# Three moves in a two-block transformer kernel: a multiply ahead of six weight splits, a weight split ahead of a routing step, and an expert's gather behind the slot scatters

## The chip, the cores and the metric

The kernel runs on one core of one Trainium2 chip. The metric is the device time of one execution in microseconds (us). Before the change it is 2412.04 us, the median of three runs (2407.6 to 2413.93).

## What is computed

Two transformer blocks follow each other on 512 tokens of width 1024, in float32. The first block has a recurrent half and an attention half whose outputs are normed and joined, a cross attention to a memory of 256 rows, and a mixture of 32 experts with two experts for each token. The second block (two layers) is not touched by the change. Cut to what matters here:

```python
y_rnn = recurrent_group(xr, xg, ...)             # gelu(xg) * h, h from a linear recurrence
y_att = chunk_band_attention(q, k, v, rel_bias)
mixed = concatenate([rms_norm(y_rnn, gn_rnn_w), rms_norm(y_att, gn_att_w)])
x = x + mixed @ w_out
x = x + memory_cross_attention(rms_norm(x, ln2_w), rms_norm(mem, mem_norm_w), xq_w, xk_w, xv_w, xo_w)
h = rms_norm(x, ln3_w)
g_p, g_idx = top_k(softmax(h @ w_group + b_group), 1)          # one of 4 groups
e_p, e_idx = top_k(softmax(logits of the 8 experts of that group), 2)
for each expert e: rows of its tokens are gathered, (silu(rows @ w_gate[e]) * (rows @ w_up[e])) @ w_down[e]
x = x + the two experts' rows of each token, weighted with g_p * e_p
```

## The kernel before, in words

Activations lie transposed, with the features on the 128 partitions and the 512 tokens along the free dimension. Each large product is made of three matmuls on a high and a low part of both operands. A weight therefore goes through a fixed chain: SyncE loads it into `ring`, ScalarE copies a high part of it, VectorE subtracts to get the low part, and only then TensorE reads it. Each engine has its own program, which is a fixed list in the order in which the code is written, and semaphores tie the lists together. An instruction that waits holds everything that is written behind it on its engine.

**The stage before the first attention.** The weights come in units of 256 columns (numbered g). `unit_high(g)` is ScalarE's copy (line 1245), `unit_low(g)` VectorE's subtraction (line 1237). Units 10 to 13 make the memory's keys, units 14 to 17 its values, units 18 and 19 are split for later. TensorE's list is here: units 10 to 13, one matmul that sums the squares of the recurrent half (`rms("gn_rnn")`, line 1976), then units 14 to 17 (`token_unit`, line 1967). ScalarE's list is: the high part of 15, two copies of results, `root(1)` that makes `rstd` of that sum (lines 2224 and 2225, with a load of a function table ahead of each), two tiles copied, then the high part of 16. VectorE's list is the low parts 12 to 19, and behind that of 16 the four multiplies of `G` by `rstd` (line 2167). These feed ScalarE's copies `high(...)` (line 2229) inside the attention. A unit's load is issued by SyncE when the low part of the unit two before it is done.

**The start of the experts.** `moe_tensor` (TensorE) computes the router's logits, turns the rows of `H`, counts the tokens of each expert in bank 6 (line 473, semaphore `routed` 3), and makes the lists of tokens in bank 7 (line 479, `routed` 4). Then it turns the rows of `X` (line 458), turns the gathered rows of expert 0 (`turn_x`, line 488, semaphore `x_turned`) and runs the blocks of the experts (`unit`, line 498). A block has four gate and up units, after the fourth of which it turns the next expert's rows. `moe_vector` (VectorE) picks the experts, waits for `routed` 3, computes each token's rank and the mask `AT_RANK` (lines 604 to 608), which the product of line 479 waits for, then takes the low part of unit 1 (`weights_low(1, 2)`, line 562) and waits for `routed` 4. Then it writes `idx` (line 612) and the slots of tokens beyond 128 for one expert (lines 615 to 641, semaphore `slots_done`). `moe_gpsimd` (GpSimd) gathers expert 0's rows into `XB` (`gather`, line 400). When these are turned it gathers those of expert 1, stores four lists (line 411), waits for `slots_done`, issues eight indirect stores of tokens (line 415), and goes on with the gathers of experts 2 and up, each when the rows of the expert before it are turned. All of GpSimd's transfers are in one queue (q0). SyncE's loads are in another (q1).

SyncE's program of this stage (`moe_sync`) loads the gate weights of expert 2 when two low parts are done (line 354, `ew_low` 2), and its up weights when four are (`ew_low` 4), with a row of final-norm weights (`FROW`, line 362) behind them.

Of the kernel before, what the change touches and what calls it, by code (L numbers as in the profile page):

```python
# [17 lines left out]
ALU = mybir.AluOpType  # L18
# [10 lines left out]
HC = HALF // P  # L29
# [6 lines left out]
EXPERTS = GROUPS * EPG  # L36
# [77 lines left out]
def build(nc, A, out):  # L114
    with ExitStack() as ctx:
        def sb(name, shape, dt=F32):
            return ctx.enter_context(nc.sbuf_tensor(name, shape, dt))
# [33 lines left out]
        rstd = sb("rstd", [P, T])  # L151
# [6 lines left out]
        def const(name, n=P):  # L158
            return konst[:, CK[name]:CK[name] + n]

        def col(name, i=0, p=P):
            return cols[0:p, C1[name] + i:C1[name] + i + 1]
# [4 lines left out]
        Q, K, G = QKVG[:, 0:4, :], QKVG[:, 4:8, :], QKVG[:, 12:16, :]  # L167
# [22 lines left out]
        a_sq, a_add, a_stat, a_rstd = sem("x_squares"), sem("x_squares_added"), sem("x_stat"), sem("x_rstd")  # L190
        a_hn, a_hi, a_lo = sem("x_normed"), sem("x_normed_high"), sem("x_normed_low")
# [59 lines left out]
        idx = sb("idx", [P, EXPERTS], U32)  # L251
# [51 lines left out]
        def e_low(u):  # L303
            return EW[u % 3][:, 4:8, :]
# [16 lines left out]
        x_turned, x_high, x_low = sem("x_turned"), sem("expert_x_high"), sem("expert_x_low")  # L321
# [66 lines left out]
        def moe_gpsimd(pool, st):  # L388
            st.do(pool.iota(ids[:, :, :], [[T, 2], [P, TT]], base=0, channel_multiplier=1))
            st.do(pool.memset(absent[:, :], ABSENT))  # L390
            st.wait()
            pool.dma_start(slot_dram[HEAD * P:DUMMY, :].rearrange("(p n) o -> p (n o)", p=P), absent[:, :]).then_inc(scattered, 16)
            pool.dma_start(routw[:, :, :], A["router_w"].rearrange("(k p) n -> p k n", p=P)).then_inc(s_rout, 16)
            pool.dma_start(routb[:, :], bass.AP(A["router_b"].tensor, 0, [[0, P], [1, NR]])).then_inc(s_rout, 16)
            pool.wait_ge(res_done, 16)
            st.do(pool.memset(XB, 0.0))
            st.wait()

            def gather(i, index):
                pool.indirect_dma_start(XB, None, rows_dram, bass.IndirectOffsetOnAxis(index, 0), bounds_check=SLOTS - 1, oob_is_err=False).then_inc(xb_landed, 16)  # L400

            def store(index):
                pool.indirect_dma_start(y_dram, bass.IndirectOffsetOnAxis(index, 0), YB[:, :, :].rearrange("p a n -> p (a n)"), None, bounds_check=SLOTS - 1, oob_is_err=False).then_inc(y_stored, 16)

            pool.wait_ge(mask_done, 3)
            pool.wait_ge(rows_stored, 16 * TT)
            gather(0, idx[:, 0:1])
            pool.wait_ge(x_turned, 1)
            gather(1, idx[:, 1:2])
            for n in range(HEAD):  # L410
                pool.dma_start(slot_dram[n * P:(n + 1) * P, :], idx[:, EXPERTS - HEAD + n:EXPERTS - HEAD + n + 1]).then_inc(scattered, 16)
            pool.wait_ge(slots_done, 1)
            for w in range(2):
                for t in range(TT):
                    pool.indirect_dma_start(slot_dram, bass.IndirectOffsetOnAxis(slots[:, w, t:t + 1], 0),
                                            ids[:, w, t:t + 1], None).then_inc(scattered, 16)
            for i in range(2, EXPERTS - 1):
                pool.wait_ge(x_turned, i)
                gather(i, idx[:, i:i + 1])
                if i >= LAG:  # L420
                    pool.wait_ge(y_a, i - LAG + 1)
                    store(idx[:, i - LAG:i - LAG + 1])
            pool.wait_ge(scattered, 16 * (2 * TT + 5))
            extra = pool.value_load(table_u[0:1, 60:61], min_val=1, max_val=OVER + 1)
            with pool.Fori(0, extra) as j:
                pool.dma_start(idx_more[:, 0:1], slot_dram[bass.ds((j + LAG) * P, P), :]).then_inc(idx_landed, 16)
                pool.dma_start(idx_more[:, 1:2], slot_dram[bass.ds(j * P, P), :]).then_inc(idx_landed, 16)
                wait_counted(pool, idx_landed, j * 32 + 32)
                wait_counted(pool, x_turned, j + EXPERTS - 1)
                gather(j, idx_more[:, 0:1])  # L430
                wait_counted(pool, xb_landed, j * 16 + EXPERTS * 16)
                wait_counted(pool, y_a, j + EXPERTS - LAG)
                store(idx_more[:, 1:2])
                wait_counted(pool, y_stored, j * 16 + (EXPERTS - LAG) * 16)
            for n in range(LAG):
                pool.dma_start(idx_more[:, 2 + n:3 + n], slot_dram[bass.ds((extra + n) * P, P), :]).then_inc(idx_landed, 16)
            wait_counted(pool, idx_landed, extra * 32 + LAG * 16)
            for n in range(LAG):
                wait_counted(pool, y_a, extra + EXPERTS - LAG + n)
                store(idx_more[:, 2 + n:3 + n])  # L440
# [114 lines left out]
        def moe_vector(dve, st):  # L555
# [4 lines left out]
            def weights_low(u, count, b=None):  # L560
                dve.wait_ge(ew_high, count)
                dve.tensor_tensor(e_low(u), e_raw(u, b), as_f32(e_high(u)), ALU.subtract).then_inc(ew_low, 1)  # L562
# [28 lines left out]
            for w in range(2):  # L591
# [7 lines left out]
            flat_hots = hots.rearrange("p w t n -> p (w t) n")  # L599
            step(dve.tensor_tensor(hot_ids.rearrange("p w t n -> p (w t) n"), flat_hots,  # L600
                                   const("slot", 2 * TT)[:, :, None].to_broadcast([P, 2 * TT, EXPERTS]), ALU.mult))
            dve.wait_ge(routed, 3)
            before = bank[6][:, 0:TT * EXPERTS].rearrange("p (t n) -> p t n", n=EXPERTS)
            step(dve.tensor_tensor(hot_rank, hots, before[:, None, :, :].to_broadcast([P, 2, TT, EXPERTS]), ALU.mult))
# [2 lines left out]
            step(dve.tensor_reduce(rank[:, :, None], flat_rank, AX.X, ALU.add))  # L607
            st.tell(dve.tensor_tensor(AT_RANK, const("count")[:, None, :].to_broadcast([P, 2 * TT, P]),
                                      rank[:, :, None].to_broadcast([P, 2 * TT, P]), ALU.is_equal), mask_done)
            weights_low(1, 2)  # L610
            dve.wait_ge(routed, 4)
            st.tell(dve.tensor_scalar(idx[:, :], bank[7][:, 0:EXPERTS], float(ABSENT), None, ALU.add), mask_done)

# [618 lines left out]
        def unit_low(dve, st, g):  # L1232

            ks, nc_ = k_chunks(g), unit_cols(g)
            w = WHL[g % 2]
            dve.wait_ge(wh_done, g + 1)
            st.tell(dve.tensor_tensor(w[:, 1, 0:ks, 0:nc_], raw_half(g)[:, :, 0:nc_], as_f32(w[:, 0, 0:ks, 0:nc_]), ALU.subtract), wl_done)  # L1237
# [805 lines left out]
        def _(dve):  # L2043
            st = Steps(dve, dve_own)
# [114 lines left out]
            dve.wait_ge(s_biasd, 32)  # L2159
            for m in range(1, HC):  # L2160
                add_squares(DC, m, HC)
            for g in range(12, 20):
                unit_low(dve, st, g)
                if g == 16:
                    dve.wait_ge(a_rstd, 2)
                    for c in range(HC):
                        st.tell(dve.scalar_tensor_tensor(G[:, c, :], G[:, c, :], col("gn_rnn", c), rstd[:, :], ALU.mult, ALU.mult), a_hn)
            dve.wait_ge(s_bias, 1)

            def inside(p):  # L2170
# [320 lines left out]
```

## Time and profile before

| | |
|---|---|
| runs, median (lowest to highest) | 2412.04 us (2407.6 to 2413.93) |
| profiled execution, its own time | 2413.93 us |
| its span, first to last instruction | 2411.8 us (2.13 us less than its time) |
| TensorE (PE) busy | 2195.8 us, 91% of the span |
| VectorE (DVE) busy | 1584.2 us, 66% |
| ScalarE (ACT) busy | 1187.5 us, 49% |
| GpSimd (POOL) busy | 205.1 us, 9% |
| mean granted TensorE clock | 0.957 of full |

All times in the rows below are microseconds from the start of the span, of one profiled execution. A row of the timeline gives start, duration, engine, line, operation, what it writes and reads, how many instructions are merged (x), and in brackets the idle time before it with what ended it. The duration of merged rows runs from the first start to the last end. PEclk is the share of the full TensorE clock that was granted. L1031 is a line of the kernel as it was before the change.

### The profile page before, as it was taken

What the parts mean: (1) busy time and instruction counts of PE and PEld (TensorE: products, weight loads), DVE (VectorE), ACT (ScalarE), POOL (GpSimd) and SP (SyncE); (2) the same over time, 40 slices, a digit from 0 to 9 for tenths busy, and PEclk for the clock granted to TensorE, in tenths of its full rate; (3) what the DMA queues carried; (4) which work ended last, traced back from release to release, by engine and by line L of the source; (5) the groups of instructions that cost most, each with busy time, mean ns of one, the idle gap of its engine ahead of it and who ended that gap; (6) DMA issues with size and microseconds to landing.
All of it is one profiled execution on the core that took longest, in us unless ns stands there. A gap on an engine that the chain in (4) does not pass through costs nothing.

```text
span 2411.8 us, 27159 instructions
## 1 busy us (share of the span) xinstructions
PE 2195.8 (91%) x10362; PEld 1741.0 (72%) x10362; DVE 1584.2 (66%) x1884; ACT 1187.5 (49%) x1437; POOL 205.1 (9%) x155
## 2 busy tenths in 40 slices
PE   6998898889999999993988989999989798999997
PEld 4786577677777787772855778888766466888885
DVE  6447543468888888885677476465568767655565
ACT  4535533357777777775466342222245554322223
POOL 1000000021111111110010011020100100211020
PEclk9998899989999999996999999999999999999998
DMA  5242031469999999975210113223222002232321
GB/s 193 91 151 97 18 123 35 179 162 362 357 359 350 356 363 357 351 290 213 73 52 17 53 70 105 88 88 107 103 87 70 36 1 76 100 105 83 109 88 53
DMA packets 48814, 359.98 MB, mean 149 GB/s; under 512 B 12224, under 2 KB 13416, under 8 KB 21456
## 3 DMA queue, kind: packets, MB, share of 16 engines
q1 hardware_dynamic: 36880, 340.89, 38.5%
q0 software_dynamic: 10752, 13.60, 1.7%
q10 hardware_dynamic: 1088, 4.19, 0.4%
q8 instruction: 64, 1.05, 0.2%
q14 instruction: 30, 0.25, 0.0%
HBM read 360.71 MB, written 25.72 MB: 160 GB/s over the span
## 4 chain that ended last, share of the span: by engine, by line
PE 76%; DVE 11%; ACT 8%; issue 4%; DMA 1%; ACTq 0%; SPq 0%; DVEq 0%; POOLq 0%
PE bank L1031 40%; PE bank L498 14%; PE bank L1942 10%; DVE split_products L562 3%; ACT split_products L726 2%; PE bank L1967 2%; PE bank L1744 1%; PE bank L488 1%; PE bank L1729 1%; ACT S L1808 1%; PE bank L1758 1%; DVE X L1282 1%; DVE split_weights L1237 1%; ACT S L1819 1%; ACT S L761 1%
## 5 line engine op out<-in xcount | busy, mean ns | idle before, releaser
L1031 PE MATMUL bank<-split_x_high,split_weights 128*128 128x512 f32 x2144 | 672.5, 394 | 31.2 <-DVE split_x_low L1251 14.7
L1245 ACT ACTIVATE split_weights<-ring 128x2048 fp32r<-128x2048 f32 (+1 forms) x122 | 228.2, 1872 | 648.2 <-PE bank L1031 526.5
L1031 PEld LDWEIGHTS bank<-split_x_high,split_weights 128*128 128x128 f32 x2144 | 407.8, 190 | 122.2 <-issue 36.8
L1237 DVE TENSOR_TENSOR split_weights<-ring,split_weights 128x2048 fp32r<-128x2048 f32 (+1 forms) x122 | 276.6, 2268 | 228.5 <-ACT split_weights L1245 228.4
L1031 PE MATMUL bank<-split_products,split_weights 128*128 128x512 f32 x1200 | 334.4, 395 | 4.5 <-DVE split_products L1437 4.5
L1031 PE MATMUL bank<-split_x_low,split_weights 128*128 128x512 f32 x800 | 312.5, 391 | 0.0
L1031 PEld LDWEIGHTS bank<-split_products,split_weights 128*128 128x128 f32 x1200 | 229.0, 191 | 53.9 <-DVE split_products L1437 6.0
L498 PE MATMUL bank<-split_products 128*128 128x512 f32 x768 | 189.7, 396 | 11.8 <-DVE split_products L562 11.8
L498 PE MATMUL bank<-split_x_low,split_products 128*128 128x512 f32 x768 | 192.4, 400 | 6.8 <-DVE split_x_low L562 4.7
L498 PE MATMUL bank<-split_x_high,split_products 128*128 128x512 f32 x768 | 190.0, 397 | 8.0 <-DVE split_x_high L562 8.0
L562 DVE TENSOR_TENSOR split_products<-ring,split_products 128x2048 fp32r<-128x2048 f32 x63 | 144.4, 2293 | 57.9 <-ACT split_products L726 52.8
L498 PEld LDWEIGHTS bank<-split_products 128*128 128x128 f32 x768 | 142.2, 188 | 53.7 <-DVE split_products L562 24.5
L1942 PE MATMUL bank<-split_x_high,split_weights 128*128 128x512 f32 x512 | 164.1, 400 | 12.5 <-DVE split_x_low L2073 7.4
L1031 PEld LDWEIGHTS bank<-split_x_low,split_weights 128*128 128x128 f32 x800 | 151.1, 189 | 31.3
L498 PEld LDWEIGHTS bank<-split_x_low,split_products 128*128 128x128 f32 x768 | 144.6, 192 | 36.8 <-DVE split_x_low L562 5.0
L498 PEld LDWEIGHTS bank<-split_x_high,split_products 128*128 128x128 f32 x768 | 143.7, 190 | 36.8 <-DVE split_x_high L562 8.2
L1009 POOL TENSOR_TENSOR QKVG<-QKVG 128x512 f32<-128x512 f32 x44 | 97.8, 2223 | 811.5 <-DVE QKVG L1451 725.0
L562 DVE TENSOR_TENSOR split_x_low<-ring,split_x_low 128x2048 fp32r<-128x2048 f32 x62 | 141.9, 2288 | 23.9 <-ACT split_x_low L726 23.9
L562 DVE TENSOR_TENSOR split_x_high<-ring,split_x_high 128x2048 fp32r<-128x2048 f32 x63 | 144.1, 2288 | 5.1 <-ACT split_x_high L726 5.1
L726 ACT ACTIVATE split_products<-ring 128x2048 fp32r<-128x2048 f32 x63 | 121.2, 1924 | 36.5 <-PE bank L498 31.2
L1942 PEld LDWEIGHTS bank<-split_x_high,split_weights 128*128 128x128 f32 x512 | 98.8, 193 | 36.1 <-issue 15.2
L726 ACT ACTIVATE split_x_low<-ring 128x2048 fp32r<-128x2048 f32 x62 | 119.1, 1920 | 5.7 <-PE bank L498 5.7
(421 smaller groups left out, 2973.4 us busy)
## 6 DMA issues: line engine op xcount, KB each, us to landing
ring<-in_expert_down_w SPq DMA_DIRECT2D x32, 2048.0 KB
ring<-in_expert_gate_w SPq DMA_DIRECT2D x31, 2048.0 KB, 8.3
ring<-in_expert_up_w SPq DMA_DIRECT2D x31, 2048.0 KB, 7.8
ring<-in_ffn_w_up SPq DMA_DIRECT2D x44, 1024.0 KB, 4.8
ring<-in_w_in SPq DMA_DIRECT2D x26, 1024.0 KB, 4.9
ring<-in_ffn_w_down SPq DMA_DIRECT2D x16, 1024.0 KB, 4.7
ring<-in_w_out SPq DMA_DIRECT2D x12, 1024.0 KB, 4.8
ring<-in_ffn_w_down SPq DMA_DIRECT2D x8, 768.0 KB, 4.1
```

The lines of the kernel that those rows point to most:

```text
L488: mm = pe.transpose(bank[4 + j][:, c * P:(c + 1) * P], XB[:, (4 * j + c) * P:(4 * j + c + 1) * P], ident)
L498: mm = pe.matmul(acc[j][:, :], xs[i][:, (u % 2) * n_k + k, :], w[:, n_j * k + j, :], start=(u % 2 == 0 and k == 0 and q == 0), stop=(u % 2 ...
L562: dve.tensor_tensor(e_low(u), e_raw(u, b), as_f32(e_high(u)), ALU.subtract).then_inc(ew_low, 1)
L726: act.activation(e_high(u), e_raw(u, b), ACT.Copy).then_inc(ew_high, 1)
L761: act.activation(YB[:, 1, :], bank[3][:, :], ACT.Copy).then_inc(y_a, 1)
L1009: st.tell(pool.tensor_tensor(QKVG[:, 14 + i, :], QKVG[:, b, :], QKVG[:, 4 + b, :], ALU.mult), f_act)
L1031: mm = pe.matmul(acc[:, :], w[:, u, k, m], x, start=first and q == 0, stop=last and q == 2)
L1237: st.tell(dve.tensor_tensor(w[:, 1, 0:ks, 0:nc_], raw_half(g)[:, :, 0:nc_], as_f32(w[:, 0, 0:ks, 0:nc_]), ALU.subtract), wl_done)
L1245: st.tell(act.activation(WHL[g % 2][:, 0, 0:ks, 0:nc_], raw_half(g)[:, :, 0:nc_], ACT.Copy), wh_done)
L1282: st.do(dve.scalar_tensor_tensor(X[:, c, :], bank[a][:, :], -1.0 / D, X[:, c, :], ALU.mult, ALU.add))
L1942: mm = pe.matmul(accs[i][:, 0:n], w[:, u, k, i * P:(i + 1) * P], x, start=(k == order[0] and q == 0), stop=(k == order[-1] and q == 2))
L1967: mm = pe.matmul(bank[(n0 + t) % 4][:, 0:256], x[:, tok], w[:, u, k, :], start=(k == 0 and q == 0), stop=(k == DC - 1 and q == 2))
```

## The change

Three edits, all of them of order. The arithmetic is the same.

```diff
             gather(0, idx[:, 0:1])
-            pool.wait_ge(x_turned, 1)
-            gather(1, idx[:, 1:2])
             for n in range(HEAD):
                 pool.dma_start(slot_dram[n * P:(n + 1) * P, :], idx[:, EXPERTS - HEAD + n:EXPERTS - HEAD + n + 1]).then_inc(scattered, 16)
             pool.wait_ge(slots_done, 1)
...
-            for i in range(2, EXPERTS - 1):
+            for i in range(1, EXPERTS - 1):
                 pool.wait_ge(x_turned, i)
                 gather(i, idx[:, i:i + 1])
...
                                    const("slot", 2 * TT)[:, :, None].to_broadcast([P, 2 * TT, EXPERTS]), ALU.mult))
+            weights_low(1, 2)
             dve.wait_ge(routed, 3)
...
                                       rank[:, :, None].to_broadcast([P, 2 * TT, P]), ALU.is_equal), mask_done)
-            weights_low(1, 2)
             dve.wait_ge(routed, 4)
...
-            for g in range(12, 20):
+            unit_low(dve, st, 12)
+            unit_low(dve, st, 13)
+            dve.wait_ge(a_rstd, 2)
+            for c in range(HC):
+                st.tell(dve.scalar_tensor_tensor(G[:, c, :], G[:, c, :], col("gn_rnn", c), rstd[:, :], ALU.mult, ALU.mult), a_hn)
+            for g in range(14, 20):
                 unit_low(dve, st, g)
-                if g == 16:
-                    dve.wait_ge(a_rstd, 2)
-                    for c in range(HC):
-                        st.tell(dve.scalar_tensor_tensor(G[:, c, :], G[:, c, :], col("gn_rnn", c), rstd[:, :], ALU.mult, ALU.mult), a_hn)
```

VectorE's list in the stage before the first attention stood like this before. The first row is the low parts of units 10 and 11, `ext<-gatew` are the sums of squares, and `QKVG` holds G:

```order
L1237 TENSOR_TENSOR split_weights<-ring,split_weights 128x2048 x2
L2157 TENSOR_TENSOR ext<-gatew 128x512
L2157 TENSOR_TENSOR ext<-ext,gatew 128x512 x2
L1237 TENSOR_TENSOR split_weights<-ring,split_weights 128x2048 x5
L2167 SCALAR_TENSOR_TENSOR QKVG<-QKVG,cols,rstd 128x512 x4
L1237 TENSOR_TENSOR split_weights<-ring,split_weights 128x2048 x3
```

The same stretch of the changed kernel:

```order
L1235 TENSOR_TENSOR split_weights<-ring,split_weights 128x2048 x2
L2155 TENSOR_TENSOR ext<-gatew 128x512
L2155 TENSOR_TENSOR ext<-ext,gatew 128x512 x2
L1235 TENSOR_TENSOR split_weights<-ring,split_weights 128x2048 x2
L2164 SCALAR_TENSOR_TENSOR QKVG<-QKVG,cols,rstd 128x512 x4
L1235 TENSOR_TENSOR split_weights<-ring,split_weights 128x2048 x6
```

The four multiplies, which wait for `rstd`, now stand ahead of the low parts of units 14, 15 and 16.

GpSimd's list at the start of the experts before (`S<-rows_scratch` is a gather, and the first row holds the gathers of experts 0 and 1):

```order
L400 DMA S<-rows_scratch,idx 128x1024 x2
L411 DMA slot_tokens<-idx 128x1 x4
L415 DMA slot_tokens<-ids,slots 2432x1 x8
L400 DMA S<-rows_scratch,idx 128x1024 x2
L403 DMA expert_rows<-S,idx 1024x1024
```

And now:

```order
L400 DMA S<-rows_scratch,idx 128x1024
L409 DMA slot_tokens<-idx 128x1 x4
L413 DMA slot_tokens<-ids,slots 2432x1 x8
L400 DMA S<-rows_scratch,idx 128x1024 x3
L403 DMA expert_rows<-S,idx 1024x1024
```

The gather of expert 1 went past four plain and eight indirect transfers, and past the wait for `slots_done`.

## Rows read from the trace of the kernel before

**Rows 1.** The page: shares of the chain that ended last, by engine.

```profile
PE 76%; DVE 11%; ACT 8%; issue 4%; DMA 1%; ACTq 0%; SPq 0%; DVEq 0%; POOLq 0%
```

**Rows 2.** Windows of the expert loop (columns: busy us by engine, PEclk, DMA share, GB/s).

```profile
core 0: us, PE busy (x) PEld busy (x) DVE busy (x) ACT busy (x) POOL busy (x), PEclk, DMA share, GB/s
532.00:1050.00 518.00, 506.95 (x2368) 412.79 (x2367) 448.03 (x284) 399.56 (x339) 58.89 (x59) 1.00 0.93 354
```

**Rows 3.** Chain of waits, 150 to 260 us: start, us, what.

```profile
180.31 23.04 PE bank L1967 x192
```

**Rows 4.** Timeline of ACT, 155 to 250 us.

```profile
179.55 1.92 ACT L1245 ACTIVATE split_weights<-ring 128x2048 fp32r<-128x2048 f32 x1 [3.30 <-PE bank L1942]
...
182.03 1.28 ACT L2224 ACT_TABLE_LOAD   x1
...
185.32 0.63 ACT L2225 ACTIVATE rstd<-rstd 128x512 f32<-128x512 f32 x1
```

**Rows 5.** Timeline of DVE, 155 to 250 us.

```profile
175.74 2.29 DVE L1237 TENSOR_TENSOR split_weights<-ring,split_weights 128x2048 fp32r<-128x2048 f32 x1 [3.47 <-ACT split_weights L1245]
...
190.31 2.73 DVE L2167 SCALAR_TENSOR_TENSOR QKVG<-QKVG,cols,rstd 128x512 f32<-128x512 f32 x4
```

**Rows 6.** Timeline of PE, 460 to 560 us: matmuls after idle time, and in the loop.

```profile
517.98 5.48 PE L498 MATMUL bank<-split_x_low,split_products 128*128 128x512 f32 x12 [4.73 <-DVE split_x_low L562]
...
526.03 2.88 PE L498 MATMUL bank<-split_products 128*128 128x512 f32 x12
...
544.20 3.06 PE L498 MATMUL bank<-split_products 128*128 128x512 f32 x12 [0.32 <-DVE split_products L562]
```

**Rows 7.** Timeline of DVE, 455 to 560 us: around the moved weight split.

```profile
482.87 0.42 DVE L604 TENSOR_TENSOR S<-nothing,bank 128x256 f32<-128x256 f32 x1 [2.21 <-PE bank L473]
...
484.92 2.28 DVE L562 TENSOR_TENSOR split_x_high<-ring,split_x_high 128x2048 fp32r<-128x2048 f32 x1
488.72 0.19 DVE L612 TENSOR_SCALAR idx<-bank 128x32 uint32<-128x32 f32 x1 [1.51 <-PE bank L479]
```

**Rows 8.** Timeline of ACT, 455 to 560 us.

```profile
480.54 1.91 ACT L726 ACTIVATE split_x_high<-ring 128x2048 fp32r<-128x2048 f32 x1 [0.44 <-ACT S L735]
```

**Rows 9.** Timeline of PE, 460 to 560 us: rows of X, the turns of experts 0 and 1.

```profile
485.06 3.62 PE L479 MATMUL bank<-S,gatew 128*128 128x32 f32 x16 [0.59 <-DVE gatew L608]
488.49 5.93 PE L458 MATMUL bank<-konst,X 128*128 128x128 f32 x32
495.90 1.06 PE L488 MATMUL bank<-konst,S 128*128 128x128 f32 x8 [1.48 <-DMA S<-rows_scratch,idx]
...
511.64 1.04 PE L488 MATMUL bank<-konst,S 128*128 128x128 f32 x8
```

**Rows 10.** Timeline of POOL, whole span.

```profile
489.82 1.11 POOL L400 DMA_INDIRECT S<-rows_scratch,idx  x1 [31.20 <-DVE idx L612]
497.75 1.02 POOL L400 DMA_INDIRECT S<-rows_scratch,idx  x1 [6.81 <-PE bank L488]
498.77 2.22 POOL L411 DMA_DIRECT2D slot_tokens<-idx  x4
501.30 1.04 POOL L415 DMA_INDIRECT slot_tokens<-ids,slots  x1 [0.30 <-issue]
...
506.49 2.33 POOL L415 DMA_INDIRECT slot_tokens<-ids,slots  x1 [0.30 <-issue]
...
511.67 0.97 POOL L415 DMA_INDIRECT slot_tokens<-ids,slots  x1 [0.31 <-issue]
...
1058.47 2.02 POOL L403 DMA_INDIRECT expert_rows<-S,idx_more  x1 [8.65 <-issue]
```

**Rows 11.** Timeline of DVE, 455 to 560 us: weight splits beside GpSimd's transfers.

```profile
493.85 2.29 DVE L562 TENSOR_TENSOR split_products<-ring,split_products 128x2048 fp32r<-128x2048 f32 x1
497.62 1.29 DVE L648 TENSOR_TENSOR split_products<-bank,split_products 128x512 fp32r<-128x512 f32 x2 [1.48 <-ACT split_products L755]
505.68 2.29 DVE L562 TENSOR_TENSOR split_x_low<-ring,split_x_low 128x2048 fp32r<-128x2048 f32 x1 [6.77 <-ACT split_x_low L726]
```

**Rows 12.** The same, 1055 to 1066 us.

```profile
1057.30 2.29 DVE L562 TENSOR_TENSOR split_products<-ring,split_products 128x2048 fp32r<-128x2048 f32 x1 [1.27 <-ACT split_products L726]
```

**Rows 13.** Timeline of SP, 484 to 520 us: loads of expert 2's weights.

```profile
487.30 0.33 SPq L354 DMA_DIRECT2D ring<-in_expert_gate_w  x1
508.07 0.33 SPq L354 DMA_DIRECT2D ring<-in_expert_up_w  x1
```

**Rows 14.** DMA issues, 508 to 518 us: KB each, us to landing.

```profile
ring<-in_expert_up_w SPq DMA_DIRECT2D x1, 2048.0 KB, 17.8
```

**Rows 15.** Window behind expert 1's gather (columns as in rows 2).

```profile
502.00:502.50 0.50, 0.50 (x3) 0.40 (x2) 0.00 (x0) 0.00 (x0) 0.34 (x1) 0.50 0.00 0
```

## The prediction

> **What bounds the kernel now.** I read the page's chain first: three quarters of it is TensorE [rows 1]. A move therefore counts where TensorE waits for what is moved, and an idle time elsewhere is worth nothing. Then I looked at the two stages that the diff touches, engine by engine, in the timelines. Before the first attention TensorE runs without a pause from 180.31 to 203.35 through the four value units [rows 3]. At the start of the experts it does pause, and each pause ends on a hand-over from another engine [rows 6, 9]. In the expert loop TensorE is busy 506.95 of 518 us with the DMA engines at 0.93 [rows 2]: nothing there is left to take up a late start, so what is lost before the loop stays lost. The profiled execution took 2413.93 us, 2.13 more than its span and 1.89 more than the median. I work out differences and add them to the median.
>
> **Part A, the four multiplies before units 14 to 19.** What is moved is short: four instructions, 2.73 us [rows 5]. What counts is what they wait for. `rstd` is ready at 185.32 + 0.63 = 185.95 [rows 4]. It can't be earlier: TensorE's sum of squares stands behind unit 13 (it is what ends at 180.31), and ScalarE does the high part of unit 15 from 179.55 and two table loads first. None of those lists is changed. VectorE before did unit 14's low part at 175.74 to 178.03, 2.28 us before TensorE took it at 180.31 [rows 3, 5]. Now this split is queued behind the wait. VectorE starts the multiplies at 186.0. The next instruction starts about 0.1 us before the last one's recorded end, so it starts at 188.65, takes 2.29, and TensorE starts unit 14 at 191.0. The stall is 191.0 - 180.3 = **10.7 us**, in the middle of a stretch without a pause. Behind it unit 15's split follows at once and is 3 us early for its turn; the loads of units 16 and 17 start later but have a unit's time to land. No other engine had been late here before, so removing the 2.73 us from its old place gives back nothing.
>
> After a pause the granted clock is low. TensorE's twelve matmuls after 4.73 us of idle took 5.48 us, and twelve at full clock 2.88 [rows 6]. I add this difference, **2.6 us**, after a pause twice as long. Part A is 13.3 us; its bounds are 10.7 (clock kept) and 15 (clock low for nearly twice as long).
>
> **Part B, the split of unit 1 ahead of the wait for `routed` 3.** ScalarE's copy ends at 482.45 [rows 8], the counts arrive for 482.87 [rows 7]. VectorE now takes the split first, 482.5 to 484.8, and the rank step starts at 484.8 and not 482.87: 1.93 us later. So are the mask, TensorE's product of 485.06, the rows of X behind it, `idx`, expert 0's gather and `slots_done` [rows 7, 9, 10]. In its old place the split lay beside that product, with 1.51 us of idle time left over: there it cost nothing. What absorbs part of the delay is the pause of 1.48 us in which TensorE waited for expert 0's rows at 495.90. TensorE ends the rows of X at 494.42 + 1.93 = 496.35. The gather is issued at 491.75, and it meets less traffic, since the gate load of expert 2 goes out 2.4 us earlier too (487.30 to 484.9) [rows 13]. From expert 1's gather I take at most 4.7 us from issue to landing: issued at 497.75, nothing more is moved from 502.0 on, and I allow 0.4 for the semaphore [rows 10, 15]. That gives 496.45. So expert 0's turn comes at 496.4: **+0.5 us**. Bounds: 0.4 (TensorE's own list excludes less) and 3, if the early gate load shares the engines with the rows that ScalarE is still storing and delays all that waits for these.
>
> **Part C, expert 1's gather behind the slot stores.** TensorE wants these rows at 511.64, with part B at 512.1 to 512.3 [rows 9]. I place GpSimd's list again. Expert 0's gather runs 491.75 to 492.85 and the four stores to 495.07. `slots_done` comes at 493.85 + 1.93 = 495.8 (VectorE's next instruction marks it) [rows 10, 11], and the first slot store starts at 496.05. The eight are 1.29 us apart, but one took 2.33 instead of about 1.0 [rows 10]. It ran from 506.49 to 508.82, while VectorE did a split of two SBUF operands until 507.97 [rows 11]. The second long one is the same picture: 1058.47 to 1060.49, against a split that ends at 1059.59 [rows 10, 12]. The gather at 497.75, beside VectorE's subtraction from a PSUM bank, took 1.02 [rows 10, 11]. So a GpSimd transfer issued under such a split is done about 0.9 us after it.
> The Trainium skill (GPSIMD Engine Reference, Specifications) says that GpSimd shares its SBUF interfaces with VectorE and contends with VectorE instructions that have two SBUF inputs. By that rule the trace agrees, with the 2.33 and 2.02 us; without it every store would count 1.0 and the gather below would go out 1.9 us earlier.
> Now the first slot store lies under the split moved to 495.8 to 498.1, and ends at 498.95. The next six end at 506.6. The eighth, at 506.95, lies under unit 3's split (505.68 + 0.5, to 508.5), and ends at 509.35. Expert 1's gather goes out at 509.65 instead of 497.75. Alone, it would land 4.7 us later, at 514.35: 2.0 us late.
>
> It isn't alone. The up load of expert 2 is issued at 508.07 + 0.5 = 508.6, a microsecond before it [rows 13]. Two rows bound what that does. Expert 0's gather was issued 2.5 us after the gate load, and its rows ended TensorE's wait at 495.90, 8.6 us after that load's issue, 6.1 after its own [rows 9, 10, 13]: by that, expert 1's rows land at 517.1, 4.8 us late. And the up load at this very place took 17.8 us to land [rows 14]: if the gather ends only with it, that is 526.4, 14.1 us late. I take **7 us**, near the first, since the size of gather and load is the same, and above it, since the place has the slow load. All of it reaches TensorE, for expert 1's first unit starts on a chain behind this turn (ScalarE's copies of rows and weights, VectorE's split: the pause before 517.98) [rows 6].
> The Trainium skill (DMA: Bandwidth & Descriptors, Queues, rings and completion order) says that a DMA engine takes turns between queues, but drains a whole packet of descriptors of one before it goes to the next. By that rule the gather waits for the load's part on each engine, as expert 0's did; the trace agrees with its 6.1 us against 4.7. The same page's fit for a GpSimd transfer, 2.0 us and the bytes at 436 GB/s, would have it there in time (an estimate of under 3 us for a gather).
> Later gathers go out a whole block before they are used; they are not moved.
>
> **Sum.** 13.3 + 0.5 + 7 = 20.8 us slower, 2412.0 + 20.8 = **2433 us**.
>
> **Rivals.**
> - *The gather is hardly late.* For it: small packets may slip between those of the load; expert 1's own took 4.7. Against it: 6.1 us for expert 0's. Part C is 0 to 2: 13.8 + 1 = 14.8, so 2427 us.
> - *The gather ends with the slow load.* For it: the 17.8 us, and the row of norm weights that is loaded behind. Against it: only one such load in the trace. Part C is 12 to 15: 13.8 + 13.5 = 27.3, so 2439 us.
> - *The multiplies cost nothing: not slower.* VectorE had 3.47 us of idle time before unit 14's split [rows 5]. If `rstd` were there in it, the multiplies would hide, and the 1.5 us pause of TensorE before 495.90 could shrink with the gate load out of the gather's way: 0 to -1 us, 2411 to 2412. It decides at one point: the multiplies and the split take 2.65 + 2.29, so `rstd` has to be ready by 175.4 for TensorE to get unit 14 by 180.3. It comes at 185.95, ScalarE and TensorE keep their lists, and the part C gather would have to be in time as well.
>
> **Chances.** The forecast (2430 to 2436 by itself) has 0.55. The gather hardly late has 0.22, the gather with the slow load 0.16, not slower 0.02. The last 0.05 is a slowdown of another size, such as part B at its upper bound. 2423 to 2440 takes in the first three cases, the bounds of the clock and most of part B's. A measurement of this kernel can tell about 0.3%, 7 us, from no change; part A alone is 10.7. So slower has 0.95, within 0.3% 0.03, faster 0.02.
>
> **What would show it.** Part A: TensorE idle 10 to 11 us before the first value unit, ended by VectorE's split of unit 14, behind four multiplies at 186, and a PEclk of 0.5 right after. Part B: the rank step behind a split, 1.9 us later relative to the counts; the turn of expert 0 only about 0.5 us later. Part C: one slot store of over 2 us under each of two splits, the gather of expert 1 about 12 us behind its old place, and a wait of TensorE on a DMA of gathered rows after expert 0's fourth unit. The forecast is wrong if TensorE doesn't wait before the value units, if the attention or the loop gets shorter, or if the loop's start is less than 14 us later than before.

## The result, and the profile after it

The changed kernel takes 2439.91 us, the median of four runs (2438.31 to 2442.5). The kernel before, run beside it, has a median of 2411.6 us. The ratio is 1.012, with a 95% interval of 1.0106 to 1.0136: 28.3 us slower. The forecast was 20.8 us slower, so 7.5 us are missing, and 2439.9 is the time of the rival "the gather ends with the slow load" (2439).

The profiled execution took 2438.64 us, with a span of 2436.5 (before 2411.8). That pair differs by only 24.7 us, because before's profile lost 3.6 us where nothing was changed. This is the same stretch of both, with the same 627 matmuls (columns as in rows 2):

```profile
1751.00:1925.00 174.00, 152.92 (x627) 106.66 (x626) 127.92 (x187) 94.46 (x131) 7.92 (x4) 0.93 0.18 63
```

```profile
1779.20:1949.60 170.40, 149.16 (x627) 104.08 (x626) 127.54 (x187) 94.35 (x131) 7.92 (x4) 0.96 0.18 65
```

The first row is before's, the second the changed kernel's. The granted clock was 0.93 against 0.96, and the stretch 174.0 against 170.4 us. Ahead of it the changed kernel is 28.2 us late, which is what the medians say. So the parts below are measured as offsets between the two traces, not as a difference of spans.

Its chain, to be read against rows 1, is still three quarters TensorE, and the share of DMA has gone from 1% to 2%:

```profile
PE 75%; DVE 10%; ACT 9%; issue 3%; DMA 2%; POOL 0%; ACTq 0%; SPq 0%; DVEq 0%; POOLq 0%
```

**Part A.** The timelines of ScalarE, VectorE and TensorE of the changed kernel, 175 to 222 us:

```profile
185.95 0.63 ACT L2224 ACTIVATE rstd<-rstd 128x512 f32<-128x512 f32 x1
```

```profile
186.61 2.74 DVE L2164 SCALAR_TENSOR_TENSOR QKVG<-QKVG,cols,rstd 128x512 f32<-128x512 f32 x4 [13.71 <-ACT rstd L2224]
189.26 4.49 DVE L1235 TENSOR_TENSOR split_weights<-ring,split_weights 128x2048 fp32r<-128x2048 f32 x2
```

```profile
179.92 1.02 PE L1974 MATMUL bank<-ext,konst 128*128 128x512 f32 x2
191.61 23.65 PE L1965 MATMUL bank<-split_weights,split_mixed 128*128 128x256 f32 x177 [10.66 <-DVE split_weights L1235]
...
219.66 0.97 PE L1727 MATMUL bank<-QKVG 64*128 64x128 f32 x8 [2.60 <-ACT MKV L2238]
```

Read them from the top: `rstd` is ready at 186.58, the multiplies follow, then the splits of units 14 and 15, and TensorE starts unit 14 after 10.66 us of idle time. The clock right behind it (columns as in rows 2):

```profile
191.00:197.00 6.00, 5.39 (x27) 5.39 (x28) 2.75 (x2) 0.00 (x0) 0.00 (x0) 0.54 0.67 265
197.00:203.00 6.00, 6.00 (x53) 6.00 (x52) 1.18 (x1) 2.46 (x3) 0.00 (x0) 1.00 0.22 87
```

27 matmuls in the first 6 us, at about the lower level of 1.2 GHz (0.54 of the full clock), and 53 in the second 6 us at 2.4 GHz. The attention starts at 219.66, against 205.94 before. Of these 13.72 us, 0.63 were there ahead of the pause (`rstd` at 185.95 against 185.32), so part A cost 13.1.

**Part B.** VectorE and TensorE of the changed kernel at the start of the experts:

```profile
497.07 2.29 DVE L560 TENSOR_TENSOR split_x_high<-ring,split_x_high 128x2048 fp32r<-128x2048 f32 x1 [1.89 <-ACT split_x_high L724]
499.28 0.41 DVE L603 TENSOR_TENSOR S<-nothing,bank 128x256 f32<-128x256 f32 x1
```

```profile
501.46 3.62 PE L477 MATMUL bank<-S,gatew 128*128 128x32 f32 x16 [2.48 <-DVE gatew L607]
504.89 6.44 PE L456 MATMUL bank<-konst,X 128*128 128x128 f32 x32
512.51 1.09 PE L486 MATMUL bank<-konst,S 128*128 128x128 f32 x8 [1.18 <-ACT AUX L746]
515.71 2.98 PE L496 MATMUL bank<-split_x_low,split_products 128*128 128x512 f32 x12 [2.10 <-DVE split_products L646]
518.53 2.88 PE L496 MATMUL bank<-split_x_high,split_products 128*128 128x512 f32 x12
521.25 2.88 PE L496 MATMUL bank<-split_products 128*128 128x512 f32 x12
523.97 2.88 PE L496 MATMUL bank<-split_x_low,split_products 128*128 128x512 f32 x12
540.96 1.97 PE L486 MATMUL bank<-konst,S 128*128 128x128 f32 x8 [14.11 <-DMA S<-rows_scratch,idx]
```

The rank step (L603) stands behind the split, and TensorE's product (L477) waits 2.48 us where it waited 0.59 [rows 9]. The turn of expert 0's rows (512.51) waits for ScalarE's copy of the rows of X, not for the gather.

**Part C.** GpSimd and SyncE of the changed kernel, same place:

```profile
510.51 2.94 POOL L413 DMA_INDIRECT slot_tokens<-ids,slots  x1 [0.98 <-DVE table_u L639]
...
521.42 2.46 POOL L413 DMA_INDIRECT slot_tokens<-ids,slots  x1 [0.30 <-issue]
524.18 1.06 POOL L400 DMA_INDIRECT S<-rows_scratch,idx  x1 [0.30 <-issue]
```

```profile
523.12 0.33 SPq L354 DMA_DIRECT2D ring<-in_expert_up_w  x1
523.50 0.42 SPq L362 DMA_DIRECT2D X<-in_final_row  x1
```

The gather goes out at 524.18. This stage starts 14.5 us late (the router's logits at 478.42 against 463.93), and the prediction's 509.65, moved by as much, is 524.15. It ends the wait at 540.9, 16.7 us later. The issues of 500 to 545 us show that the load beside it was as slow (KB, us to landing):

```profile
ring<-in_expert_up_w SPq DMA_DIRECT2D x1, 2048.0 KB, 16.5
...
slot_tokens<-ids,slots POOLq DMA_INDIRECT x8, 7.3
```

Behind this wait the offset to before is 29.3 us (expert 3's rows are turned at 579.12 against 549.82). At the end of the loop it is 28.8 (1075.68 against 1046.84), and 28.2 at the untouched stretch above.

### The profile page after: what moved, and what is told of

Its sections match the earlier page's. It is cut to its first block, busy times and chain, and to the rows that moved or that the text cites. A ratio compares the mean times of both kernels' runs of the same rounds, so it can differ in the third digit from the quotient of the medians.

```text
span 2436.5 us, 27159 instructions
## 1 busy us (share of the span) xinstructions
PE 2192.2 (90%) x10362; PEld 1740.6 (71%) x10362; DVE 1583.9 (65%) x1884; ACT 1187.4 (49%) x1437; POOL 207.2 (9%) x155
## 4 chain that ended last, share of the span: by engine, by line
PE 75%; DVE 10%; ACT 9%; issue 3%; DMA 2%; POOL 0%; ACTq 0%; SPq 0%; DVEq 0%; POOLq 0%
PE bank L1029 39%; PE bank L496 15%; PE bank L1940 10%; DVE split_products L560 3%; ACT split_products L724 2%; PE bank L1965 2%; PE bank L1742 1%; PE bank L486 1%; PE bank L1756 1%; ACT S L1806 1%; PE bank L1727 1%; DVE split_weights L1235 1%; DVE X L1280 1%; ACT S L759 1%; DMA S<-rows_scratch,idx 1%
## 5 line engine op out<-in xcount | busy, mean ns | idle before, releaser
L1940 PE MATMUL bank<-split_x_high,split_weights 128*128 128x512 f32 x512 | 164.4, 401 | 12.4 <-DVE split_x_low L2071 7.3
L724 ACT ACTIVATE split_x_high<-ring 128x2048 fp32r<-128x2048 f32 x63 | 120.7, 1916 | 2.5 <-DMA ring<-in_expert_down_w 2.0
```

What stands on the lines that cost most here:

```text
L724: act.activation(e_high(u), e_raw(u, b), ACT.Copy).then_inc(ew_high, 1)
L1940: mm = pe.matmul(accs[i][:, 0:n], w[:, u, k, i * P:(i + 1) * P], x, start=(k == order[0] and q == 0), stop=(k == order[-1] and q == 2))
```

## Experiments

Each ran beside the kernel before on the same chip. "+x" is the difference of the medians. The ratio is worked out from the single runs and is not the quotient of the medians: it gives 12.8 us and not 10.2 for the wait alone, and 31.6 and not 28.9 for the stores away from the load. Both values lie in the interval. Single executions also differ ahead of anything edited: at the router's logits the traces below that have their edits only behind it are -0.1 to 4.6 us late against before's. So offsets in a trace are taken from there.

**The multiplies alone.**

```diff
             for g in range(12, 20):
                 unit_low(dve, st, g)
-                if g == 16:
+                if g == 13:
                     dve.wait_ge(a_rstd, 2)
```

> Only the four multiplies are moved, ahead of the weight splits of units 14 to 16. Theory 1 (a stall behind the wait for rstd, and nothing taken up later): TensorE idle 10.7 us before the first value unit, about 2.4 us more from the low clock behind it, time 13 to 14 us above before. Theory 2 (part of the stall is taken up by the attention or the experts): the idle time is the same 10.7 us, but the time is less than 9 us above before.

2426.24 us, ratio 1.0063 (1.0043 to 1.0084), +13.9. Its TensorE has the same pause:

```profile
190.25 25.21 PE L1967 MATMUL bank<-split_weights,split_mixed 128*128 128x256 f32 x192 [10.66 <-DVE split_weights L1237]
```

Part A is what was forecast, and by itself.

**The wait alone, the multiplies in their old place.**

```diff
                 unit_low(dve, st, g)
+                if g == 13:
+                    dve.wait_ge(a_rstd, 2)
                 if g == 16:
                     dve.wait_ge(a_rstd, 2)
```

> The multiplies stay behind the split of unit 16, and only the wait for rstd is put ahead of the split of unit 14. If the wait is what costs, as I predicted, TensorE is idle 8.0 us (10.7 less the 2.65 us of the multiplies) and the time is 9 to 12 us above before. If the multiplies' own work is what costs, it is idle less than 3 us and the time is within 4 us of before.

2419.70 us, ratio 1.0053 (1.0034 to 1.0072), +10.2. TensorE:

```profile
189.01 25.18 PE L1967 MATMUL bank<-split_weights,split_mixed 128*128 128x256 f32 x192 [8.01 <-DVE split_weights L1237]
```

8.01 of the 10.66 us are there without any of the moved work. The multiplies are the other 2.65.

**The multiplies one unit later** (`g == 14`).

> The wait and the multiplies stand one unit later than in the change, between the splits of units 14 and 15. Unit 15 is due at 186.07, and its split now ends at 186.0 + 2.65 + 2.29 = 190.95: TensorE idle 4.9 us, ahead of unit 15 instead of unit 14, and with the low clock behind it 5 to 7.5 us above before. The rival (the wait moves a stall about without making it smaller) has it idle 10 us or more.

2417.97 us, ratio 1.0038 (1.0022 to 1.0055), +8.4. TensorE:

```profile
180.33 6.31 PE L1967 MATMUL bank<-split_weights,split_mixed 128*128 128x256 f32 x48
191.56 19.98 PE L1967 MATMUL bank<-split_weights,split_mixed 128*128 128x256 f32 x144 [4.93 <-DVE split_weights L1237]
```

Unit 14 is done in the meantime, so the pause is one unit (about 5.7 us) shorter: 4.93. The time is a little above the 5 to 7.5 us that were expected; the interval (5.3 to 13.3 us) doesn't tell the two apart. Two units later it should be gone, which the last experiment shows.

**The weight split alone.**

```diff
+            weights_low(1, 2)
             dve.wait_ge(routed, 3)
...
-            weights_low(1, 2)
             dve.wait_ge(routed, 4)
```

> Only the split of expert unit 1 is moved ahead of the wait for the token counts. Theory 1: the rank step is 1.9 us later and so is TensorE's turn of expert 0's rows (1.9 to 2.1 us), because the last copy of the X rows on ScalarE, not the gather alone, stood right before it; a different clock behind the pause can give 1 to 2 us back: time 0 to 3 us above before. Theory 2 (my prediction: the pause on the gather takes up all but 0.5 us): the turn of expert 0 is 0.5 us later relative to the router's product.

2412.83 us, ratio 1.0004 (0.9994 to 1.0013), +0.5. TensorE:

```profile
500.18 1.09 PE L488 MATMUL bank<-konst,S 128*128 128x128 f32 x8 [1.17 <-ACT AUX L748]
503.37 2.97 PE L498 MATMUL bank<-split_x_low,split_products 128*128 128x512 f32 x12 [2.10 <-DVE split_products L648]
```

As in the changed kernel the turn waits for ScalarE's copy. The twelve matmuls behind it took 2.97 us. Before they took 4.58:

```profile
499.06 4.58 PE L498 MATMUL bank<-split_x_low,split_products 128*128 128x512 f32 x12 [2.10 <-DVE split_products L648]
```

The turn is 2.1 us later relative to the router's logits (500.18 and 466.08, against 495.90 and 463.93 before), and 1.6 come back from the clock: 1.00 of full was granted over these twelve matmuls, 0.63 before, after the same 2.10 us of idle time. Why it was granted here stays open. The size is as forecast, the way to it isn't.

**The gather behind the stores, alone** (the first part of the diff, without the other two).

> Only expert 1's gather is moved behind the slot stores. Theory 1 (the gather is issued about a microsecond behind the up load of expert 2 and lands with it, and that load is slow, 17.8 us): GpSimd issues it at about 507.5 to 508, TensorE waits 13 to 15 us for the rows after expert 0's fourth unit, time 13 to 16 us above before. Theory 2 (in the changed kernel the delay needs the shifts of the other two edits, because without them the gather goes out before the load): the gather is issued before or with the load at 508 and lands 4.7 us later, TensorE waits less than 3 us, time less than 4 us above before.

2423.19 us, ratio 1.0046 (1.003 to 1.0063), +10.8. TensorE:

```profile
522.83 1.97 PE L486 MATMUL bank<-konst,S 128*128 128x128 f32 x8 [10.44 <-DMA S<-rows_scratch,idx]
```

The gather's issue began at 506.98, ahead of the up load (508.65). It lay under a weight split of VectorE (506.26 to 508.55), took 2.51 us and ended at 509.49, behind the load's. The last store was issued at 505.71. The load took 13.5 us here, and the gather landed 0.6 us after it. The wait is above the 7 I had taken, and shorter than the 14.1 in the changed kernel: it lies between the two theories.

**The same, with the row of norm weights loaded later.**

```diff
-            sp.dma_start(FROW, A["final_row"].to_broadcast([P, D])).then_inc(s_const, 16)
             down(1, 1)
+            sp.dma_start(FROW, A["final_row"].to_broadcast([P, D])).then_inc(s_const, 16)
```

> Expert 1's gather is moved as in the run before, and the row of final-norm weights, which SyncE loads right behind the up load of expert 2, is loaded behind the down load of expert 1 instead, some 25 us later. Theory R (the 128-fold read of one row of HBM makes the up load and the gather slow): the up load lands in 8 to 9 us, the gather too, TensorE waits 2 to 6 us instead of 13 to 15. Theory S (the up load is slow for another reason, such as the eight stores of 4-byte tokens): the up load still needs 16 to 18 us and the wait stays 13 to 15 us.

2420.85 us, ratio 1.004 (1.0029 to 1.0051), +8.5. TensorE waits 8.95 us and the load takes 12.4:

```profile
520.97 1.97 PE L486 MATMUL bank<-konst,S 128*128 128x128 f32 x8 [8.95 <-DMA S<-rows_scratch,idx]
```

The load lies between the 8 to 9 and the 16 to 18 us of the two theories. Without the row the wait is at most 1.5 of 10.4 us shorter ("at most", because the last store was also 0.4 us further ahead of the load). The row is not what makes the load slow.

**The token stores away from the load.** The gather stays where it was before the change; one of the eight indirect stores goes out behind the gather of each of the experts 5 to 12.

```diff
-            pool.wait_ge(slots_done, 1)
-            for w in range(2):
-                for t in range(TT):
-                    pool.indirect_dma_start(slot_dram, ...)
             for i in range(2, EXPERTS - 1):
                 pool.wait_ge(x_turned, i)
                 gather(i, idx[:, i:i + 1])
...
+                if 5 <= i < 13:
+                    w, t = divmod(i - 5, TT)
+                    pool.wait_ge(slots_done, 1)
+                    pool.indirect_dma_start(slot_dram, ...)
```

> The kernel before, with the eight indirect stores of tokens taken out of the start of the experts and issued one at a time behind the gathers of experts 5 to 12. Theory W (the thousand 4-byte writes to HBM make the up load of expert 2 slow): that load, issued at about 508, lands in 8 to 9 us instead of 17.8. Theory T (the load is slow for another reason): it still needs 12 us or more. In both the time is within 3 us of before, since TensorE does not wait for that load.

2438.42 us, ratio 1.0131 (1.0114 to 1.0148), +28.9. The load of the disputed place took 7.9 us and not 17.8 [rows 14]:

```profile
ring<-in_expert_up_w SPq DMA_DIRECT2D x1, 2048.0 KB, 7.9
```

So the stores make it slow. The price in the loop was not expected: the time was to stay within 3 us. DMA issues of 590 to 745 us, first before, then this kernel:

```profile
GB/s 363 303 421 334 383 422 262 365 358 381 371 294 356 406 365 328 326 326 423 383 266 376 350 397 426 250 362 350 393 381 289 335 395 399 326 322 314 414 384 272
...
ring<-in_expert_up_w SPq DMA_DIRECT2D x8, 2048.0 KB, 8.3
```

```profile
GB/s 281 411 412 414 313 80 263 441 420 330 63 216 428 417 408 159 43 300 430 366 365 179 97 310 420 430 423 203 114 421 365 402 310 72 258 425 418 354 59 178
...
ring<-in_expert_up_w SPq DMA_DIRECT2D x7, 2048.0 KB, 14.3
```

This kernel's GB/s row (40 slices of 3.9 us) dips to 43 to 114 once in each block, where before's never falls under 250, and the up loads land 6 us later. The waits of this kernel from 560 to 745 us follow (us in total, times, longest):

```profile
PE bank L498 <- DVE split_products L562: 11.7, 6, 3.7
...
ACT split_x_low L726 <- DMA ring<-in_expert_gate_w: 9.9, 4, 3.9
ACT split_products L726 <- DMA ring<-in_expert_up_w: 9.8, 5, 3.2
...
PE bank L498 <- DVE split_x_low L562: 9.1, 3, 3.7
```

ScalarE waits for late gate and up loads nine times, and TensorE behind it for the splits, nine times and 20.8 us in all.

Eight stores of 512 bytes each cost 28.9 us by the medians, 3.6 us a store. The trace bears it out: the turns of the experts' rows come later from store to store, 25.6 us late behind the eighth (741.12 against 715.49, and 759.51 against 733.92), 3.2 us a store, and no further.

**The gather beside the load, without the stores.** The gather of expert 1 waits also for `ew_low` 4, which releases the up load, so that the two meet in any case. This kernel leaves out the eight indirect stores (which matter only where an expert has more than 128 tokens), the next all but four of them.

```diff
-            pool.wait_ge(x_turned, 1)
-            gather(1, idx[:, 1:2])
...
             pool.wait_ge(slots_done, 1)
-            for w in range(2):
-                for t in range(TT):
-                    pool.indirect_dma_start(slot_dram, ...)
+            pool.wait_ge(x_turned, 1)
+            pool.wait_ge(ew_low, 4)
+            gather(1, idx[:, 1:2])
...
```

> Leaves out the eight indirect stores of tokens (which matter only where an expert has over 128 tokens), and holds expert 1's gather until unit 3's low part is done, which is also what lets SyncE issue the up load of expert 2. So gather and load go out together at about 508, as in the changed kernel, but with no small writes about. Theory W (small writes to HBM make load and gather slow): the load lands in 8 to 9 us, the gather at about 517, TensorE waits 4 to 6 us, time 4 to 6 us above before. Theory M (the meeting alone makes it slow): the wait is 9 us or more, as with the stores.

2417.36 us, ratio 1.0019 (1.0009 to 1.0029), +5.6. The load took 8.3 us. TensorE:

```profile
517.16 1.97 PE L485 MATMUL bank<-konst,S 128*128 128x128 f32 x8 [5.60 <-DMA S<-rows_scratch,idx]
```

**The same with four stores ahead.**

> The same with the first four of the eight stores left in. They are issued from about 494 to 501 and so are over well before the load at 508. Theory W1 (the writes are still being worked off when the load comes, in proportion to their number): the load lands in 10 to 11 us and TensorE waits 6 to 9 us. Theory W2 (only a store that is issued within 2 to 3 us of the load slows it): as with no stores, 8 to 9 us and a wait of 4 to 6 us.

2419.37 us, ratio 1.0029 (1.0019 to 1.004), +7.6. The last store went out at 504.56, the load 8.2 us later, at 512.76, and it took 8.4 us. TensorE waits 5.77:

```profile
522.28 1.97 PE L489 MATMUL bank<-konst,S 128*128 128x128 f32 x8 [5.77 <-DMA S<-rows_scratch,idx]
```

Stores that have landed (the last one took 7.9 us, to 512.5) do nothing to the load. What counts is whether they are still under way. The GB/s of 25 us around the load, in 40 slices of 0.625 us, shows it. The changed kernel from 520 us, the load issued at 523.12:

```profile
GB/s 1 0 1 0 0 0 341 52 26 0 0 0 79 52 52 0 0 79 446 419 419 420 452 308 66 249 269 216 118 131 112 111 46 7 0 0 0 0 0 0
```

Without stores, from 505 us, the load issued at 507.79:

```profile
GB/s 0 0 0 0 0 0 367 131 341 393 419 446 400 446 393 295 380 315 125 20 0 0 0 0 0 0 66 52 190 138 7 0 0 0 0 0 0 0 0 0
```

With stores the load begins, then almost nothing moves for some 7 us (slices 8 to 18, at most 79 GB/s), and then it runs at over 400 GB/s. Without them it runs at once. Before the change the picture of this load was the same, with the rows of expert 1 already there (from 505 us, issued at 508.07):

```profile
GB/s 1 0 1 0 0 0 236 131 52 0 0 0 26 79 26 52 52 341 446 419 420 446 341 138 184 138 20 46 98 92 86 20 197 85 302 157 20 0 0 0
```

**The gather after three of the eight stores.**

```diff
+                    if w * TT + t == 3:
+                        pool.wait_ge(x_turned, 1)
+                        gather(1, idx[:, 1:2])
                     pool.indirect_dma_start(slot_dram, ...)
```

> Expert 1's gather is issued between the third and the fourth of the eight indirect stores. If the loss is the meeting with the up load, as I think, the gather goes out at about 500.6, lands by 505.5, TensorE does not wait for it, and the time is within 3 us of before. If the loss is that it stands behind the stores in GpSimd's queue (each store slow to be done), TensorE waits for it even so, and the time is 4 us or more above before.

2412.51 us, ratio 1.0018 (1.0008 to 1.0027), +3.0. The gather goes out at 501.79 and TensorE turns its rows without a wait:

```profile
513.45 1.03 PE L489 MATMUL bank<-konst,S 128*128 128x128 f32 x8
```

The load took 16.1 us, and no one minded: it is slow wherever stores are under way, and it only matters when the gather is beside it. The move doesn't make the 3.0 us. This trace is 1.84 us late at the router's logits, ahead of the move (465.77 against 463.93), and 1.84 in the loop (606.88 against 605.04). And the kernel before had a median of 2409.54 beside this one and of 2411.77 beside the next, which has the same order on GpSimd.

**Two of the moves, to places where nothing waits.** The gather as above, the multiplies after unit 15 (`g == 15`). The weight split stays where it was.

> The multiplies go behind the split of unit 15 (one unit before their place in the kernel before), and expert 1's gather between the third and fourth token store; the weight split of expert unit 1 stays. Unit 16 is due at 191.8 and its split can end at 186.0 + 2.65 + 2.29 = 190.95, but needs ScalarE's high part of unit 16 (done at 188.1), so it ends at about 191.0, 0.8 us early. TensorE has no pause there, and none on the gather: time within 3 us of before. If my account of either place misses a wait, it is 5 us or more above.

2411.56 us, ratio 0.9999 (0.999 to 1.0008), −0.2. VectorE, then TensorE:

```profile
186.18 2.74 DVE L2168 SCALAR_TENSOR_TENSOR QKVG<-QKVG,cols,rstd 128x512 f32<-128x512 f32 x4 [2.20 <-ACT rstd L2226]
188.84 2.28 DVE L1238 TENSOR_TENSOR split_weights<-ring,split_weights 128x2048 fp32r<-128x2048 f32 x1
```

```profile
179.94 23.59 PE L1968 MATMUL bank<-split_weights,split_mixed 128*128 128x256 f32 x192
...
511.69 1.04 PE L489 MATMUL bank<-konst,S 128*128 128x128 f32 x8
```

VectorE still waits 2.20 us for `rstd`, but nothing late is queued behind it. The moves cost nothing there; they also bring nothing.

## Why the prediction was half right

- **What bounds.** Right: what was lost ahead of the expert loop stayed lost (29.3 us at its start, 28.8 at its end).
- **Part A**, forecast 13.3, measured 13.1 in the pair of traces and 13.9 alone. The stall was 10.66 against 10.7, the clock 2.4 against 2.6. The reason was right too: the wait by itself makes 8.01 of it.
- **Part B**, forecast +0.5, measured +0.5 alone and +0.7 in the pair of traces. The step behind it failed: "What absorbs part of the delay is the pause of 1.48 us". Before the change, ScalarE's last copy of the rows of X ended at 495.54, and the turn started at 495.90. Only 0.36 us were free, and in the changed kernel the turn is 16.6 us late (512.51 against 495.90), while the router's logits of the same stage start 14.5 us late (478.42 against 463.93): 2.1 us more. That the size came out is luck: the forecast didn't have the 1.6 us that the clock gave back.
- **Part C, the place of the gather.** Right: two long transfers under VectorE's splits, the gather at 524.18 against 524.15. The 2.94 us one (510.51 to 513.45) lies under the split of 510.26 to 512.55, the 2.46 us one under the split that starts at 520.74. The Trainium skill (GPSIMD Engine Reference, Specifications) has GpSimd contend with VectorE instructions that read two SBUF inputs; the trace agrees for an issue that begins under such a split and is done about 0.9 us behind it, with 1.96 to 2.95 us in the runs of this stage, against 0.96 to 1.11 elsewhere. It doesn't for one that begins just ahead of a split: the store of 508.29, in the kernel with the weight split alone, took 0.97 us beside a split from 508.38. One sum of the prediction is wrong here: without the contention the gather would go out 3.3 us earlier and not 1.9, for both long stores count (2.9 and 2.4 us instead of 1.0).
- **Part C, its landing.** This step failed: "I take **7 us**, near the first, since the size of gather and load is the same, and above it, since the place has the slow load." It was 14.1, and these 7.1 us are nearly all of the 7.5 that are missing. The two bounds, 4.8 and 14.1, were not two rules with the truth between them, but one rule with two lengths of the load. Expert 0's gather had landed 0.8 us after the gate load beside it (issued at 487.30, DMA issues of before, 486 to 496 us):

```profile
ring<-in_expert_gate_w SPq DMA_DIRECT2D x1, 2048.0 KB, 7.8
```

In all five kernels in which expert 1's gather met the up load, it landed 0.2 to 1.3 us after that load. So the first bound is the price of a meeting with a normal load (4.8 forecast, 5.60 and 5.77 measured). But the load at the place in question was not normal, its 17.8 us stood in the rows, and I weighed that row by size and not by what stood around it. It was slow because eight small stores were under way (7.9 to 8.4 us without them). The gather moves behind exactly these stores, so it had to meet the slow load. The right value was the upper bound. That it fits to 0.1 us is luck: the load took 16.5 us and not the 17.8 taken, and the gather landed 1.3 us after it and not with it.
- **Interplay.** The three parts alone add up to 13.9 + 0.5 + 10.8 = 25.2 us, together they cost 28.3. The medians alone are too wide to tell these 3 us, but the traces show them: the wait is 14.11 against 10.44 us, and the load took 16.5 against 13.5. Over all kernels the load is slower where the last store is issued later, with only the two near 16 us out of order (us, minus is ahead of the load):

| kernel | last store, from the load's issue | load lands after |
|---|---|---|
| weight split alone | +4.9 | 19.1 |
| before, and the three with only the multiplies or their wait moved | +3.6 | 17.6 to 18.4 |
| two moves, harmless places | -1.5 | 16.8 |
| gather after three stores | -1.6 | 16.1 |
| changed | -1.7 | 16.5 |
| gather alone | -2.9 | 13.5 |
| the same, row later | -3.4 | 12.4 |
| four stores ahead | -8.2 | 8.4 |
| no stores near | | 7.9, 8.3 |

Parts A and B shifted the stores against the load, from 2.9 to 1.7 us ahead of it, and that fits the 3 us. No run makes this shift by itself.
- **What stays open in part C.** The stores hold up the gather itself too. In the last kernel of the experiments it stood behind three of them with no load under way (issued at 500.15, the up load at 508.11) and landed after 8.8 us, against 4.7 at most without stores ahead of it. By that, with no load at all, it would have landed at 533.0 in the changed kernel and not at 540.9, some 6 us late (an estimate). No run has it behind all eight stores without the load.

What in a store holds up the loads stays open. The Trainium skill (DMA: Bandwidth & Descriptors, Anatomy of one DMA) says that a transfer's semaphore is written only after its last write is confirmed, and that this is slowest where the target is HBM. The trace agrees in direction: a store of 512 bytes to HBM takes 7.3 us to land, expert 0's gather into SBUF only 3.6 in the same kernel (issued at 506.23). That the data of other queues pause meanwhile is not in that sentence. Stores of larger pieces, or to SBUF, were not tried.

## What to carry to other kernels

A wait is moved together with everything queued behind it: look up when what it waits for is ready, and how early the next instruction of that engine was before; a split that was 2.28 us early can't stand behind a wait that ends some 6 us after the split is due. When a transfer moves, don't price it by transfers of its size, but by the one that already runs where it is going, and ask why that one is slow. And when two rows give two bounds, see first whether one rule gives both: then the truth is at one of them and not between. Small indirect stores belong where no load is under way that somebody waits for, never one in each block of a loop that runs on its loads (3.6 us each here).

## What was not expected of the hardware

- Eight indirect stores of 128 x 4 bytes slow a 2048 KB load from 7.9 to 8.4 us to 12.4 to 19.1 while they are under way, with the data at 0 to 79 GB/s for some 7 us in the changed kernel. In the loop they cost 3.6 us each.
- A gather of about 0.2 MB issued within 1 us of a 2048 KB load lands only after that load, 8.5 to 8.7 us after its issue and 5.6 to 5.8 us late for its turn, though no store is under way and it is alone in its queue.
- Two executions of kernels with the same untouched stretch differed by 3.6 us in it, by the granted clock alone (0.93 and 0.96). A pair of profiles can be that far from the pair of medians.
